# Level masks moved from GpSimd to VectorE in the merged stage of a two-layer hybrid decoder, with an early output weight, one range clear and a new order table

## What is computed

```python
def rwkv_time_mix(proj, prev, s0, lp):
    p = proj.astype(f32)
    shifted = jnp.concatenate([prev.astype(f32)[:, None], p[:, :-1]], axis=1)
    xs = p + (shifted - p) * lp["rwkv_mu"].astype(f32)      # the token "mix"
    ...
def wkv_scan(r, decay, k, v, a, b, s0):
    def step(s, inp):
        r_t, w_t, k_t, v_t, a_t, b_t = inp
        sa = jnp.einsum('bhvk,bhk->bhv', s, a_t)
        s = s * w_t[:, :, None, :] + sa[..., None] * b_t[:, :, None, :] + v_t[..., None] * k_t[:, :, None, :]
        return s, jnp.einsum('bhvk,bhk->bhv', s, r_t)
```

## Time and profile before

| | us |
|---|---|
| median of 3 runs (range) | 2237.69 (2234.87 to 2243.52) |
| the profiled execution | 2238.46 |
| its span, first to last instruction | 2236.7 |
| PE busy | 1968.3 (88%) |
| DVE busy | 1227.9 (55%) |
| ACT busy | 713.1 (32%) |
| POOL busy | 144.9 (6%) |

### The profile page before, as it was taken

One profiled execution on the slowest core, in us unless ns is written; L12 is line 12 of the kernel. 1 busy time (PEld: TensorE's weight loads), 2 busy tenths in 40 slices (PEclk: granted clock), 3 DMA queues, 4 the chain that ended last, 5 costly groups with the idle time before them and its releaser, 6 DMA issues.

```text
span 2236.7 us, 53867 instructions
## 1 busy us (share of the span) xinstructions
PE 1968.3 (88%) x22324; PEld 1810.8 (81%) x22324; DVE 1227.9 (55%) x2006; ACT 713.1 (32%) x1310; POOL 144.9 (6%) x229
## 2 busy tenths in 40 slices
PE   5999899888786999999579987998897969999994
PEld 5998778766585999999469986887575859999994
DVE  3344778887536444452343457788875364444423
ACT  3222333433333222242133222433333332222421
POOL 0000120111000000000000001201110000000000
PEclk8998799999897999999789987999998979999997
DMA  4325433133321223223132254232333212223231
GB/s 176 95 76 163 116 108 112 59 106 99 90 95 44 90 95 95 90 88 98 34 137 87 75 182 132 82 106 60 100 97 106 80 39 95 90 91 95 85 96 69
DMA packets 155838, 214.38 MB, mean 96 GB/s; under 512 B 21570, under 2 KB 121411, under 8 KB 153923
## 3 DMA queue, kind: packets, MB, share of 16 engines
q1 hardware_dynamic: 151682, 208.64, 30.1%
q10 hardware_dynamic: 3904, 2.23, 0.3%
HBM read 202.57 MB, written 16.59 MB: 98 GB/s over the span
## 4 chain that ended last, share of the span: by engine, by line
PE 61%; DVE 22%; SPq 7%; issue 4%; DMA 3%; ACT 2%; DVEq 0%; ACTq 0%
PE ps L803 17%; PE ps L805 16%; PE ps L804 16%; SPq L699 5%; PE ps L1129 2%; DVE hf_lo L1653 1%; DMA out_shift<-arena 1%; DVE arena L1956 1%; DVE arena L1965 1%; DVE arena L1960 1%; PE ps L1095 1%; DVE x L2143 1%; PE ps L1102 1%; DVE arena L1963 1%; DVE smp L2000 1%
## 5 line engine op out<-in xcount | busy, mean ns | idle before, releaser
L1646 DVE TENSOR_TENSOR ring_lo<-ring,ring_hi 128x1024 fp32r<-128x1024 f32 x202 | 247.5, 1226 | 699.6 <-ACT ring_hi L1283 699.5
L803 PE MATMUL ps<-hm_hi,ring_hi 128*128 128x260 f32 x1664 | 474.8, 285 | 28.4 <-DVE hm_lo L1653 28.4
L805 PE MATMUL ps<-hm_hi,ring_lo 128*128 128x260 f32 x1664 | 472.9, 284 | 0.0
L804 PE MATMUL ps<-hm_lo,ring_hi 128*128 128x260 f32 x1664 | 471.6, 283 | 0.0
L1283 ACT ACTIVATE ring_hi<-ring 128x1024 fp32r<-128x1024 f32 x202 | 213.9, 1059 | 698.9 <-PE ps L805 677.1
L803 PEld LDWEIGHTS ps<-hm_hi,ring_hi 128*128 128x128 f32 x1664 | 316.5, 190 | 31.5 <-issue 31.5
L804 PEld LDWEIGHTS ps<-hm_lo,ring_hi 128*128 128x128 f32 x1664 | 316.2, 190 | 0.0
L805 PEld LDWEIGHTS ps<-hm_hi,ring_lo 128*128 128x128 f32 x1664 | 316.1, 190 | 0.0
L803 PE MATMUL ps<-in_hi,ring_hi 128*128 128x260 f32 x800 | 231.6, 289 | 13.6 <-DVE in_lo L1653 13.6
L805 PE MATMUL ps<-in_hi,ring_lo 128*128 128x260 f32 x800 | 227.8, 285 | 0.0
L804 PE MATMUL ps<-in_lo,ring_hi 128*128 128x260 f32 x800 | 227.7, 285 | 0.0
(11 more groups left out here) (388 smaller groups left out, 3330.0 us busy)
## 6 DMA issues: line engine op xcount, KB each, us to landing
ring<-in_w SPq DMA_DIRECT2D x202, 512.0 KB, 3.5
arena<-in_kv_cmp SPq DMA_DIRECT2D x96, 128.0 KB, 2.4
extra<-in_kv_cmp SPq DMA_DIRECT2D x80, 128.0 KB, 2.3
slot<-in_kv_cmp SPq DMA_DIRECT2D x80, 128.0 KB, 2.2
out_win_old<-in_win SPq DMA_DIRECT2D x16, 511.0 KB, 4.1
slot<-in_k_sel SPq DMA_DIRECT2D x96, 64.0 KB, 1.9
arena<-in_k_sel SPq DMA_DIRECT2D x96, 64.0 KB, 1.9
extra<-in_v_sel SPq DMA_DIRECT2D x96, 64.0 KB, 1.9
```

The lines of the kernel that those rows point to most:

```text
L803: mmul(out, wh, hi[:, k, cols], start=(k == 0), stop=False)
L804: mmul(out, wh, lo[:, k, cols], start=False, stop=False)
L805: last = mmul(out, wl, hi[:, k, cols], start=False, stop=(ci == len(chunks) - 1 and k == k1 - 1))
L1646: v.tensor_tensor(ring_lo[:, n % RING, :], r, ring_hi[:, n % RING_HI, :], SUB).then_inc(S["w_lo"], 1)
```

## The change

The level masks `lev` are now stored transposed for all levels (`levt`). `inv` multiplies the unmasked `gb` with `ww`, and the mask is laid on the product when it leaves PSUM: `qmask`, a VectorE multiply of 128x512, takes the place of ScalarE's `qcopy`. GpSimd's masks `mm` go, and so do their waits. `dif` is computed by VectorE for all four chunks, as a step of its own. `cdone` and `heads` go from VectorE to ScalarE. GpSimd has nothing left in the merged stage.

The places of the units are renumbered (units 0 and 2 are loaded before the input projection is over, unit 1 after it), the nine transfers of the gates move behind unit 3, and `ssel` and `pt_s` change sides in `smp`. The first output chunk `C_OUT` is loaded after unit 31 and split in the merged stage (`early`: `whi` on ScalarE, `wlo` on VectorE); the next two are loaded when `sel_out` of the second half is done instead of at `smp_done`. The 127 clears become one clear of a range. `ORDER` is a new string with one more digit (the `early` thread).

```diff
@@ rwkv_threads @@
+        put("dif", "DVE", 4.25)
...
-            put(("qcopy", lv), "ACT", 0.72, *here(("inv", lv)))
+            put(("qmask", lv), "DVE", 0.84, *here(("inv", lv)))
...
@@ att_thread @@
-        put(t, "cdone", "DVE", 1.43, (t, "cturn"))
+        put(t, "cdone", "ACT", 1.3, (t, "cturn"))
...
@@ early_thread @@
+    return [(("early", 0, "whi"), "ACT", 1.15, [("smp", 6, "sel_v")]), (("early", 0, "wlo"), "DVE", 1.4, [("early", 0, "whi")])]
...
-ORDER = ("055067570055550060605076067655665650006666565656666556505656566565660655705060605065050716161617156516561561551166756015"
+ORDER = ("008887660760067076677678606070760777767766077686760777770068707677007070666086001716777761761111677167116777767811617776"
...
@@ SP @@
             def host_meet(arrive, sems):
                 sp.wait_ge(arrive, 4)
-                for s in sems:
-                    sp.sem_clear(s)
+                sp.sem_clear(range(sems[0].num, sems[-1].num + 1))
...
-                for u in range(USLOT - 1):
+                for u in (0, 2):
                     load_unit(sp, mybir.EngineType.SP, l, u)
-                sp.wait_ge(S["gate_ev"], 1)
-                sp.dma_start(gate_s[:], gates[0:DEC, NQ, :].rearrange("b (h n) -> b h n", n=3)).then_inc(S["gs_ready"], 16)
...
-                for u in range(USLOT - 1, N_UNIT):
+                load_unit(sp, mybir.EngineType.SP, l, 1)
+                for u in range(USLOT, N_UNIT):
                     load_unit(sp, mybir.EngineType.SP, l, u)
+                    if u == USLOT:
+                        sp.wait_ge(S["gate_ev"], 1)
...
+                    if u == U_SV + USLOT:
+                        sp.wait_ge(S["ss_mm"], MM_AT["sel_turn1"])
+                        chunk(C_OUT)
...
+                sp.wait_ge(S["ss_mm"], MM_AT["sel_out1"])
+                for n in range(C_OUT + 1, C_OUT + RING):
+                    chunk(n)
                 sp.wait_ge(S["smp_done"], 1)
-                for n in range(C_OUT, C_OUT + RING):
-                    chunk(n)
...
@@ TensorE @@
-                        pe.wait_ge(*at_sc("mm_ok", lv))
+                        pe.wait_ge(*at_sc("gmask", 2))
...
-                                last = mmul(ps[r, 2, cj * CH:(cj + 1) * CH], mm[r, lv % 2, cj, :], ww[r, c, j, :], start=True, stop=True)
+                                last = mmul(ps[r, 2, cj * CH:(cj + 1) * CH], gb[r, c, j, 0, :], ww[r, c, j, :], start=True, stop=True)
...
@@ ScalarE @@
+                    if step == "cdone":
+                        act.wait_ge(S["at_mm"], 2 * n + 2)
+                        for half in range(2):
+                            o.go(A(pcp[0:NCP, 4 * half:4 * half + 4, :], ps[0:NCP, 4 + half, :].rearrange("p (h n) -> p h n", h=4), ACT.Copy))
+                        o.tell(S["pcp_ok"])
+                    elif step == "heads":
+                        act.wait_ge(S["pv"], FIRST[n + 1])
+                        o.go(A(hm[:, 0:PER, n * P:(n + 1) * P], b4(7), ACT.Copy))
+                        o.tell(S["o_ev"])
...
-                split_w(C_OUT, C_OUT + 1)
+                split_w(C_OUT + 1)
...
@@ VectorE @@
+                    if stage == "dif":
+                        o.do(v.tensor_tensor(dif, pr[:, :, sc * SC:(sc + 1) * SC], pr[:, :, sc * SC + 1:(sc + 1) * SC + 1], SUB))
+                        o.go(v.tensor_tensor(dif, dif, wide(C("mu"), SC), MUL))
...
+                    elif stage[0] == "qmask":
+                        lv = stage[1]
+                        dve.wait_ge(*at_sc("inv_q", lv))
+                        lo = CONST["levt"][0] + lv * CH
+                        o.go(v.tensor_tensor(q8, bank8(2), cst[:, lo:lo + CH].unsqueeze(1).to_broadcast((P, 2 * RJ, CH)), MUL))
+                        o.tell(T["inv_qc"])
```

More of the change, by code:

```diff
@@ L123, in constants @@
            for i in range(LEVELS)]
-    put("lev", two(np.concatenate(lev, 1).astype(np.float32)))
-    put("lev0t", two(lev[0].T.astype(np.float32)))
+    put("lev0", two(lev[0].astype(np.float32)))
+    put("levt", two(np.concatenate([m.T for m in lev], 1).astype(np.float32)))
     q = np.arange(SEQ).reshape(NQ, P).T
@@ L169, in rwkv_threads @@
         put = into(front)
-        put("mix", "DVE", 0.7, *([ago("rkv")] if sc else []))
+        put("dif", "DVE", 4.25)
         if sc == 0:
-            key, engine, us, _ = front.pop()
-            front.append((key, engine, us, [("rs", 0, "out")]))
+            front[-1][3].append(("rs", 0, "out"))
+        put("mix", "DVE", 0.85, *([ago("rkv")] if sc else []))
         put("tanh", "ACT", 1.05, *here("mix"))
@@ L233, in rwkv_threads @@
         put("vroot", "ACT", 0.75, *here("vrec"))
-        put("out", "DVE", 4.2, *here("vroot"))
+        put("out", "DVE", 3.8, *here("vroot"))
     return [front, back, side, tail]
@@ L267, in att_thread @@
         if t:
-            put(t - 1, "heads", "DVE", 0.84, (first - 1, "values"))
+            put(t - 1, "heads", "ACT", 0.75, (first - 1, "values"))
         put(t, "cexp", "ACT", 0.53, (t, "cmask"))
@@ L282, in att_thread @@
     put(last, "values", "PE", 0.5 + 0.17 * w, (last, "evac"))
-    put(NQ - 1, "heads", "DVE", 0.84, (last, "values"))
+    put(NQ - 1, "heads", "ACT", 0.75, (last, "values"))
     return out
@@ L300, in sample_thread @@
             put(name, b, engine, us)
-    for name, engine, us in (("c_scores", "PE", 2.4), ("c_max", "DVE", 0.44), ("c_exp", "ACT", 0.6), ("c_weigh", "DVE", 1.0),
-                             ("c_same", "PE", 0.8), ("c_impt", "DVE", 0.8), ("c_imp", "PE", 4.3), ("c_top", "DVE", 3.9)):
+    for name, engine, us in (("c_scores", "PE", 1.6), ("c_max", "DVE", 0.44), ("c_exp", "ACT", 0.6), ("c_weigh", "DVE", 1.0),
+                             ("c_same", "PE", 0.8), ("c_impt", "DVE", 0.8), ("c_imp", "PE", 2.6), ("c_top", "DVE", 3.9)):
         put(name, 0, engine, us)
@@ L345, in load_thread @@
                 last_use[a[1]] = key
[L346 to L356 removed]
+    us = [0.0, 4.5, 0.0] + [0.55 * n + 1.2 if n > 1 else 4.5 for n in UNIT_DMAS[USLOT:]]
@@ L359, in merged_order @@
 def merged_order():
     smp = sample_thread()
-    rows = (step_thread(), *rwkv_threads(), att_thread(), smp, load_thread(smp))
+    rows = (step_thread(), *rwkv_threads(), early_thread(), att_thread(), smp, load_thread(smp))
     at, order = [0] * len(rows), []
@@ L510, in build @@
         gb = at(2, RJ, 2, CH)
-        mm = at(2, 2 * RJ, CH)
+        where[0] += 1024
         rh = at(RJ, CH)
@@ L709, in host_meet @@
                 sp.wait_ge(arrive, 4)
-                for s in sems:
-                    sp.sem_clear(s)
+                assert sorted(s.num for s in sems) == list(range(sems[0].num, sems[-1].num + 1))
+                sp.sem_clear(range(sems[0].num, sems[-1].num + 1))
                 for e in go:
@@ L1511, in _ @@
                         one_step(step)
+                    elif side == "early":
+                        if step == "whi":
+                            act.wait_ge(S["u_used"], U_SV + 7)
+                            split_w(C_OUT)
                     else:
                         (rwkv if side == "rwkv" else att)(n, step)
-                split_w(C_OUT, C_OUT + 1)
+                split_w(C_OUT + 1)
                 act.wait_ge(S["mixed"], 1)
@@ L1945, in att @@
                         o.tell(S["pc_ok"])
-                    elif step == "cdone":
-                        dve.wait_ge(S["at_mm"], 2 * n + 2)
-                        for half in range(2):
-                            o.go(v.tensor_copy(pcp[0:NCP, 4 * half:4 * half + 4, :], ps[0:NCP, 4 + half, :].rearrange("p (h n) -> p h n", h=4)))
-                        o.tell(S["pcp_ok"])
                     elif step == "mask":
@@ L1966, in att @@
                         o.tell(S["sc_v"])
-                    elif step == "heads":
-                        dve.wait_ge(S["pv"], FIRST[n + 1])
-                        o.go(v.tensor_copy(hm[:, 0:PER, n * P:(n + 1) * P], b4(7)))
-                        o.tell(S["o_ev"])
                 R = slice(0, ROWS)
@@ L2122, in _ @@
                         one_step(step)
+                    elif side == "early":
+                        if step == "wlo":
+                            split_w(C_OUT)
                     else:
```

87 lines of the change are left out of this document (32 added, 55 removed).

## The result

| | before | after |
|---|---|---|
| median (range), first comparison | 2238.50 us (2234.87 to 2243.52), 4 runs | 2207.21 us (2200.14 to 2211.75), 4 runs |
| ratio after / before | | 0.986, 95% interval 0.9837 to 0.9883 |
| the same again in experiment 9 | | 0.9841, 95% interval 0.9828 to 0.9854 |
| span of the profiled execution | 2236.7 us | 2210.0 us |
| DVE busy, ACT busy, POOL busy | 1227.9, 713.1, 144.9 us | 1230.9, 702.2, 49.2 us |

The account below looks back on a forecast made before the run. TensorE and VectorE were taken to bind the merged stage first, then SP's issue of `k_sel` and `v_sel` units. -15.2 - 2 x 7 - 2 x 1.95 = -33.1 us gave a median of 2204.5 us, range 2191 to 2221.

Parts of the forecast that it names:

- The sum: Whole kernel: all terms together save 33.1 us, giving a median of 2204.5 us.
- The step from the beginning and VectorE's balance to an earlier tail: Merged stage: 5.8 us from earlier weights plus 4.4 us on VectorE start SP's tail 10 us earlier per layer.
- VectorE's balance: Ahead of SP's tail: +4.5 us of added work against 13.4 of stalls, -8.9, half counted: -4.4 us.
- The 3 us that the tail was to give back: SP's tail: VectorE steps sometimes late, costing 3 us, so the stage ends 7 us earlier per layer.
- The clears: End of each layer: one range clear replaces 127 single ones, saving 7.6 us per layer, 15.2 in all.
- The beginning: Start of merged stage: compression weights issued ahead of the gates' transfers, 5.8 us earlier per layer.
- The stall: Merged stage before the tail: small VectorE instructions held up beside GpSimd's differences, 13.4 us per layer given back.
- The end: End of merged stage: from `sel_out` to the output projection 7.1 us instead of 9.05, -1.95 us per layer.
- The tail: Merged stage's last part: SP's fifteen units still need 159.3 us and set the end; VectorE rises to 141 us.
- The rival that VectorE becomes the bound: Merged stage: VectorE fills up and the 7 us per layer go; median 2218.6 us, chance 0.17.
- The masks queue: Levels wait in VectorE's order: unchanged time at 0.8 us per level, 2249 us at 1.1; chance 0.08.

Follow-up runs that it names:

- experiment 9: The changed kernel unaltered, timed a second time on the same chip as three further variants: 2206.77 us, ratio 0.9841 to the kernel before.
- experiment 8: Changed kernel with four unused 128x1024 GpSimd multiplications added after the preparation of chunks 0 to 2: 2231.54 us, ratio 0.9951.
- experiment 3: Kernel before with GpSimd's two difference operations per chunk left out, its masks kept: 2211.65 us, ratio 0.9881.
- experiment 11: Changed kernel with the level mask left out, ScalarE copying the product scaled by zero instead: 2205.51 us, ratio 0.9837.
- experiment 5: Changed kernel with the shift store on its own semaphore, so `scaled` waits only for the state's store: 2195.56 us, ratio 0.9791.
- experiment 6: Changed kernel with two order-table digits exchanged, putting `sel_out` ahead of the last chunk's values: 2202.26 us, ratio 0.9823.
- experiment 10: Changed kernel with every VectorE mask product made twice per level: 2226.47 us, ratio 0.9925.
- 12: Changed kernel with the order table of before and ScalarE's copy in place of VectorE's mask product: 2214.15 us, ratio 0.9879.

## Why the prediction was right, and where it was not

**The sum** was 2204.5 against 2207.2, but of its parts two were confirmed and three were off, and the errors cancelled; that the sum came so close is partly luck. The step from the beginning and VectorE's balance to an earlier tail, 10 us, was near: 8.3 and 9.6 us. The 3 us that the tail was to give back did not show (+0.6 and -1.1 us), and the 1.95 us of the end were not gained.

**The clears**: -15.2 forecast, -16 measured (-10.5 to -21.5). Right in mechanism and size. What had been taken for the same 30 ns is 244 ns, and it does not matter.

**The beginning**: the forecast let all 5.8 us per layer pass to SP's tail. TensorE's first sample product does start 5.3 us earlier after the input projection (196.18 - 188.41 = 7.8, before 13.0 by the earlier trace rows), and 2 us reach the end. The step that failed is that this gain passes in full to the `k_sel` units and adds to VectorE's. Where the rest is lost is not shown.

**The stall**: 13.4 per layer forecast, 13.3 measured, and its price shown again by putting a like one back (10.7 us of stretch, 10 to 12 us of time). The Trainium skill names the cause, in GPSIMD Engine Reference, section 1 (Specifications): GpSimd's access to SBUF is shared with VectorE, with contention for VectorE's instructions in a two-port mode or with two inputs from SBUF. The trace of experiment 8 agrees in the main: in the burst shown, two-input instructions out of SBUF take up to 2.00 us instead of 0.42, and between them those with an input from PSUM keep their 0.69. Two rows are not covered by the two-input half of it: a TENSOR_SCALAR with one input is held too (3.19 us in the earlier trace rows; whether in a two-port mode no row says), and a two-input one of 128x248 in the first burst, at 283.90, keeps its 0.42.

**VectorE's balance**: here the largest term was mis-sized. The forecast priced VectorE by its busy time, +4.5 - 13.4 = -8.9 ahead of the tail, and then took half for TensorE's sake. Measured one by one, the stall counted in full (experiment 3), and taking the masks' 13.8 us per layer off again was worth nothing (experiment 11). That should have given more than the 8.3 us read at the `k_sel` units, and up to the wait at `scaled` it did.

**What was missing**: the question of what is late next. Before, VectorE reached `scaled` at 281.80 - 3.49 = 278.31, 91.1 us after the input projection's end; now at 276.37 - 10.50 = 265.87, 77.5 us after it. It is 13.6 us earlier. The line of before, from VectorE's timeline:

```profile
281.80 0.17 DVE L1861 COPY extra<-arena 128x8 f32<-128x8 f32 x1 [3.49 <-DMA out_shift<-arena]
```

It was in the trace that the forecast was made from, 3.49 us of a store that lands 13.5 us after its issue, and I did not read it. The store is now issued only 5.4 us earlier after the projection (263.97 - 188.41 against 268.18 - 187.25) and takes 12.3, so VectorE leaves 88.0 us after the projection, 6.6 earlier instead of 13.6. Seven microseconds per layer went there, and experiment 5 takes 5.6 of them back.

**The end**: -1.95 per layer forecast. The term itself held, 9.05 to 6.86 us from `sel_out`. But the forecast took `sel_out` to follow `sel_v` as before, and the new table puts the last values between. From the end of `sel_v` it is +2.3 us in layer 1 and -0.7 in layer 2, and +2.5 and +1.3 in the trace of experiment 9: nothing gained, rather something lost. Experiment 6 gets back what had been forecast (-1.1 and -2.1 against before).

**The tail**: SP bound it, 159.85 us against 159.3, and VectorE, forecast at 141 us there, had 135.1. The rival that VectorE becomes the bound is out: taking 13.8 us per layer from it changes nothing (experiment 11), and putting as much on it leaves the fifteen units as they were (experiment 10). The Trainium skill (Perfetto Trace Analysis, section Optimizing Scalar/DVE Operations) says that moving work to ScalarE may make sense where VectorE is saturated; no saturation shows here, and moving the copy back to ScalarE gains nothing.

**The masks queue** was the rival with the right mechanism and too small a chance for a reason that I did not see: I argued from the pace of the levels in the old trace, but whether the masks queue is decided by the table. In the old order they do, at 56 / 40 = 1.4 us per level (the masks' own work included), and the kernel is slower than before (2265.9; the rival had 2249 at 1.1 us). In the new one they don't. The forecast gave the order table no term of its own; here the table decides the sign. The new table on the kernel before was not run; experiments 11 and 12 put its worth at 8.6 us where ScalarE copies.

**What stays open.** The three gains measured alone on the kernel before sum to 47 us, and the changed kernel has 31 to 36. Experiments 5 and 6 account for 11 and 4 us of what it loses. How the six differences per layer that VectorE took over (2.03 us each), the twelve copies that it gave away, the places of the units and the early weight chunk divide the rest was not tried separately, and the gains need not add.

## What to carry to other kernels

When a step moves from an engine that was free to one with a full in-order queue, the time of the instruction is the small part: ask what stands behind it while it waits for its input, and give it a new place in the order, or the same change turns from a gain into a loss. When a stall goes, look at the next wait on that engine in the trace of before, even one of 3 us: it grows by what was gained. And let stores that guard different memory count on different semaphores, since the slower one is paid by both.

## What the hardware showed unexpectedly

- The smaller of two stores is the slower: the state's store of 1024 KB lands in 4.5 us, the shift's of 63 KB in 12 to 13.5. It is issued 0.6 us behind the big one on the same queue, but even from the landing of that one (267.93) it takes until 276.27, 8.3 us. From 262 to 280 us 2016 packets are under 512 B, which would be 32 B each for this store; that the small packets make it slow was not tried. From the DMA view of the changed kernel:

```profile
out_wkv_s<-arena ACTq DMA_DIRECT2D x2, 1024.0 KB, 4.5
...
out_shift<-arena ACTq DMA_DIRECT2D x2, 63.0 KB, 12.2
```

- A range clear over 127 semaphores takes 244 ns; 127 single ones take 30 ns each and as long again between them.
- A small VectorE instruction can last as long as the GpSimd operation beside it: one on 128x4 numbers takes 3.19 us beside a difference of 3.18, and one on 128x254 takes 2.00 us beside a multiplication of 8.25 / 4 = 2.06 us.
